# A hybrid decoder layer on one core: in which order of tokens the S5 gating path keeps its rows

## The reference

```python
proj = x @ w_in[l]
q, fz, iv, g, u = jnp.split(proj, ...)
o_a, sa = hgrn2_mixer(q, fz, iv, g, ...)          # gated linear recurrence, 4 heads
# inside s5_mixer, after the scan over the complex diagonal states:
y = y.reshape(B, T, D_S5) + d_skip * u
y = jax.nn.gelu(y, approximate=False)
o_b = y * jax.nn.sigmoid(y @ w_glu)
mix = jnp.concatenate([o_a, o_b], axis=-1) @ w_out[l]
x = layer_norm(ALPHA * x + mix, ln1_g[l], ln1_b[l])
x = layer_norm(ALPHA * x + conv_ffn(x, ...), ln2_g[l], ln2_b[l])
```

## Time and profile before

| what | value |
|---|---|
| median of 3 runs | 1214.69 us |
| the profiled execution, its own time | 1211.78 us |
| its span (first to last instruction) | 1210.1 us |
| granted TensorE clock, mean | 0.997 |
| TensorE busy | 97% of the span |
| VectorE busy | 67% |
| ScalarE busy | 42% |

### The profile page before, as it was taken

The page is one execution under the profiler, slowest core; times in us unless marked ns, Lnnn a source line. Parts: engine busy times, 40 slices in busy tenths (PEclk is TensorE's granted clock), DMA queues, the critical chain, the costliest instruction groups (busy, mean ns, idle before and its releaser), DMA issues.

```text
span 1210.1 us, 24082 instructions
## 1 busy us (share of the span) xinstructions
PE 1172.3 (97%) x9716; PEld 1129.5 (93%) x9716; DVE 815.3 (67%) x1517; ACT 509.1 (42%) x852; POOL 167.8 (14%) x138
## 2 busy tenths in 40 slices
PE   7999999998898999999999999999999999999996
PEld 7988889997787999998999999999999999999995
DVE  6995777657877557799627863686458743886555
ACT  5411212436755535765414541354225522554335
POOL 4210000100000233300210021001200020001452
PEclk9999999999999999999999999999999999999999
DMA  8431333528334410411272227222631265122512
GB/s 294 120 119 49 90 93 104 177 72 208 117 101 184 176 36 1 166 42 42 72 281 88 56 64 271 94 68 54 242 128 54 56 204 180 40 73 55 193 46 96
DMA packets 84815, 139.31 MB, mean 115 GB/s; under 512 B 26360, under 2 KB 52504, under 8 KB 84696
## 3 DMA queue, kind: packets, MB, share of 16 engines
q1 hardware_dynamic: 84704, 137.77, 35.7%
HBM read 97.89 MB, written 40.03 MB: 114 GB/s over the span
## 4 chain that ended last, share of the span: by engine, by line
PE 86%; DVE 8%; ACT 3%; issue 2%; DMA 1%; SPq 0%; ACTq 0%; DVEq 0%
PE psum L1905 31%; PE psum L1600 15%; PE psum L1877 15%; PE psum L1988 6%; PE psum L1619 6%; PE psum L1674 4%; PE psum L1589 1%; DVE XL L2137 1%; DVE R L2504 1%; PE psum L1727 1%; PE psum L1709 1%; DVE wl L2552 1%; PE psum L1722 1%; PE psum L1794 1%; PE psum L1795 1%
## 5 line engine op out<-in xcount | busy, mean ns | idle before, releaser
L1905 PE MATMUL psum<-XH,wh 128*128 128x258 f32 x640 | 181.3, 283 | 1.7 <-ACT ub L1305 1.4
L1905 PE MATMUL psum<-XH,wl 128*128 128x258 f32 x640 | 181.0, 283 | 0.0
L1905 PE MATMUL psum<-TR,wh 128*128 128x258 f32 x640 | 180.9, 283 | 0.0
L1905 PE MATMUL psum<-XL,wh 128*128 128x258 f32 x640 | 179.9, 282 | 0.0
L1551 POOL TENSOR_TENSOR wl<-raw,wh 128x512 fp32r<-128x512 f32 (+2 forms) x36 | 57.9, 1612 | 567.7 <-ACT wh L1254 557.1
L1877 PE MATMUL psum<-AH,wl 128*128 128x344 f32 x384 | 123.1, 320 | 0.0
L1877 PE MATMUL psum<-AL,wh 128*128 128x344 f32 x384 | 123.1, 320 | 0.0
L1905 PEld LDWEIGHTS psum<-XH,wh 128*128 128x128 f32 x640 | 121.0, 189 | 2.2 <-issue 2.2
L1877 PE MATMUL psum<-AH,wh 128*128 128x344 f32 x384 | 122.9, 320 | 0.0
L1905 PEld LDWEIGHTS psum<-XL,wh 128*128 128x128 f32 x640 | 121.5, 190 | 0.1
L1905 PEld LDWEIGHTS psum<-XH,wl 128*128 128x128 f32 x640 | 120.9, 189 | 0.0
(11 more groups left out here) (390 smaller groups left out, 2798.2 us busy)
## 6 DMA issues: line engine op xcount, KB each, us to landing
raw<-in_w_up SPq DMA_DIRECT2D x44, 512.0 KB, 3.9
ub<-rscr SPq DMA_DIRECT2D x16, 516.0 KB, 5.0
rscr<-ub SPq DMA_DIRECT2D x16, 516.0 KB, 3.9
raw<-in_w_dn SPq DMA_DIRECT2D x32, 256.0 KB, 3.2
raw<-in_w_units SPq DMA_DIRECT2D x15, 512.0 KB, 4.6
fscr<-st SPq DMA_DIRECT2D x10, 516.0 KB, 3.3
R<-in_xT SPq DMA_DIRECT2D x8, 516.0 KB, 6.6
RS<-rscr SPq DMA_DIRECT2D x8, 516.0 KB, 4.6
```

The source lines that it names most:

```text
L1905: ins = nc.tensor.matmul(psum[:, bank, 0:QW], a[:, k * P:(k + 1) * P], x, start=(start and p_ == 0), stop=(stop and p_ == 2), skip_group_c ...
```

## The change

y, the sigmoid's result and their product now stay in step order, and so do XH and XL rows 0 to 3 while they hold y. The copy `gelu c`, the split `gl c` and the product `z c` read and write runs of 128 contiguous values. The step from step order to token order is made in `zh c` and `zl c`, which each become two instructions: 1024 values read with 512 bytes from one to the next, and the 8 sample values.

```diff
-        ys = [x[:, :].rearrange("p (t n) -> p n t", t=L) for x in (*st, ybuf)]
+        ys = [x[:, :].rearrange("p (t n) -> p t n", t=L) for x in (*st, ybuf)]
...
+        def by_step(ap):
+            return ap.rearrange("p (t n) -> p t n", t=L)
+        def token_order(ap):
+            return ap.rearrange("p (t n) -> p n t", t=L)
+        def as_tokens(ap):
+            return ap.rearrange("p (n t) -> p n t", t=L)
...
                 elif kind == "zh":
                     act.wait_ge(z_ready, c + 1)
-                    me(act.activation(XH[:, HEADS + c, :], zb[c], ACT.Copy), z_hi)
+                    me(act.activation(as_tokens(XH[:, HEADS + c, 0:TP]), token_order(zb[c][:, 0:TP]), ACT.Copy))
+                    me(act.activation(XH[:, HEADS + c, TP:T], zb[c][:, TP:T], ACT.Copy), z_hi)
...
-                    me(act.activation(XH[:, c, 0:TP].rearrange("p (n t) -> p n t", t=L), ys[c][:, NS:NS + NL, :], ACT.Copy))
-                    me(act.activation(XH[:, c, TP:T], ys[c][:, 0:NS, 0], ACT.Copy), g_hi)
+                    me(act.activation(by_step(XH[:, c, 0:TP]), ys[c][:, :, NS:NS + NL], ACT.Copy))
+                    me(act.activation(XH[:, c, TP:T], ys[c][:, 0, 0:NS], ACT.Copy), g_hi)
...
             def z_split(m):
                 dve.wait_ge(z_hi, m + 1)
-                me(split(XL[:, HEADS + m, :], zb[m], XH[:, HEADS + m, :]), z_lo)
+                me(split(as_tokens(XL[:, HEADS + m, 0:TP]), token_order(zb[m][:, 0:TP]), as_tokens(XH[:, HEADS + m, 0:TP])))
+                me(split(XL[:, HEADS + m, TP:T], zb[m][:, TP:T], XH[:, HEADS + m, TP:T]), z_lo)
...
-                    me(split(n_t(XL[:, c, 0:TP]), ys[c][:, NS:NS + NL, :], n_t(XH[:, c, 0:TP])))
-                    me(split(XL[:, c, TP:T], ys[c][:, 0:NS, 0], XH[:, c, TP:T]), g_lo)
+                    me(split(by_step(XL[:, c, 0:TP]), ys[c][:, :, NS:NS + NL], by_step(XH[:, c, 0:TP])))
+                    me(split(XL[:, c, TP:T], ys[c][:, 0, 0:NS], XH[:, c, TP:T]), g_lo)
...
-                    me(TT(n_t(zb[m][:, 0:TP]), ys[m][:, NS:NS + NL, :], n_t(zb[m][:, 0:TP]), ALU.mult))
-                    me(TT(zb[m][:, TP:T], ys[m][:, 0:NS, 0], zb[m][:, TP:T], ALU.mult), z_ready)
+                    me(TT(by_step(zb[m][:, 0:TP]), ys[m][:, :, NS:NS + NL], by_step(zb[m][:, 0:TP]), ALU.mult))
+                    me(TT(zb[m][:, TP:T], ys[m][:, 0, 0:NS], zb[m][:, TP:T], ALU.mult), z_ready)
```

More of the change, by code:

```diff
@@ L2415, in _ @@
                     dve.wait_ge(g_hi, c + 1)
-                    n_t = lambda a: a.rearrange("p (n t) -> p n t", t=L)
-                    me(split(n_t(XL[:, c, 0:TP]), ys[c][:, NS:NS + NL, :], n_t(XH[:, c, 0:TP])))
-                    me(split(XL[:, c, TP:T], ys[c][:, 0:NS, 0], XH[:, c, TP:T]), g_lo)
+                    me(split(by_step(XL[:, c, 0:TP]), ys[c][:, :, NS:NS + NL], by_step(XH[:, c, 0:TP])))
+                    me(split(XL[:, c, TP:T], ys[c][:, 0, 0:NS], XH[:, c, TP:T]), g_lo)
                 elif kind == "ml":
```

## The result

| | before | after |
|---|---|---|
| median of 19 runs each | 1212.66 us | 1215.16 us |
| ratio, 95% interval | | 1.0023 [1.0014, 1.0031] |
| profiled execution, its own time | 1211.78 us | 1216.15 us |
| its span | 1210.1 us | 1214.4 us |
| its mean granted clock | 0.997 | 0.993 |

The change makes the kernel 0.23% slower, about 2.5 us in the medians. 1214.1 us was forecast and 1215.16 came, inside the range, but the step from before was off: +0.9 us was worked out and +2.5 came.

A forecast was written before the change was run, and what follows sets the result against it. TensorE, busy 97% of the span, was taken to bound the kernel; -2.0 (entry) + 1.05 (`zh 1`) + 0.9 (`zl 2`) + 0.95 (`zh 3`, `zl 3`) = +0.9 on 1213.2 gave 1214.1 us, range 1209.5 to 1219.0.

The forecast's parts named there:

- Prices: Per-instruction costs on ScalarE and VectorE: `gelu` 1.06 us, `gl` and `z` 1.23, strided `zh` and `zl` 2.1.
- The fifth rival: Runs of 128 don't read faster, so the entry gains nothing: about +4.4 us, 1217.6 us; 5% chance.
- the fourth: Rival: strided reads at 512 bytes' distance far dearer, 4.2 us a pair: +9.3 us, 1222.5 us; 5% chance.
- The VectorE terms: VectorE's strided-against-contiguous costs, nil by the skill's rule; forecast went by the trace, 2066 against 1233 ns.
- The entry: 311 to 337 us: shorter `gelu 2` and `gelu 3` bring TensorE's wait for K and later work 2.0 us earlier.
- 1.05 given back by `zh 1`: 354 to 373 us: strided `zh 1` in ScalarE's unbroken chain delays TensorE's RMS wait at 364.82 by 1.05 us.
- 0.9 given back by `zl 2`: 354 to 373 us: strided `zl 2` costs 0.9 us more, leaving the XH row 6 part level with before.
- 0.9 lost by `zh 3` and `zl 3`: 373 to 386 us: both strided, they delay level 6 and bring `kt 3` at 385.6 instead of 384.71.
- the rival in which the end hides it: Cheaper strided `zh 3` or slack in level 6 keeps the gain: down to -2.0, 1211.2 us; 10% chance.
- a second fall: Rival: wider TensorE gaps from 371 to 386 us drop the clock there too: +2.6 us, 1215.8 us; 15% chance.
- the clock is spared: Rival: shorter gaps before 335 us avoid the clock fall near 337 us: -0.8 us, 1212.4 us; 25% chance.
- The range: 1209.5 to 1219.0 us, from cases 1211.2 to 1215.8, run scatter 2.2 either side and strided-price bounds of 1.2.

The follow-up runs named there:

- e11: The changed kernel run again, unedited, beside runs of the kernel before; mean +2.6 us over before, ratio 1.0021.
- e5: The changed kernel with only `zl` contiguous as before, `zh` strided; mean +0.7 us over the kernel before, ratio 1.0007.
- e6: The changed kernel with only `zh` contiguous as before, `zl` strided; mean +0.5 us over the kernel before, ratio 1.0009.
- e2: The kernel before with only `zh` and `zl` made strided in two instructions; mean +7.5 us over before, ratio 1.0059.
- e7: The changed kernel with the last strided split, `zl 3`, on GpSimd instead of VectorE; mean +0.6 us over the kernel before, ratio 1.0006.
- e1: The changed kernel with both `zh` and `zl` contiguous as before (entry alone); mean -2.2 us against the kernel before, ratio 0.998.
- e9: The changed kernel with the return to token order made in `z`, `zh` and `zl` contiguous; mean -1.7 us against before, ratio 0.9988.
- e8: The changed kernel with throwaway matmuls ahead of level 7 of head 3 and `kt 3`; mean +1.6 us over before, ratio 1.0009.

## Why the prediction was right or wrong

- **Prices.** Right, for all six kinds of instruction, to 0.1 us. The fifth rival (runs of 128 don't read faster) and the fourth (dearer at 512 bytes) fall with them. The VectorE terms are not nil either: its strided split takes 2041 ns and its contiguous one 1219.
- **The entry, -2.0 us.** -2.27 in the table of stretches, -2.28 again in e11. It came out of three waits and not only out of the one for K that was named: K from 1.58 to 0.60 us, the wait of 0.68 us for level 7's QP at 327.35 to nothing, and one called "issue" near 320 us from 1.36 to 0.85. K did not come at 329.7 but at 331.63, since a fall near 303 us and the start had put 2.2 us in front of it; the RMS product and `kt 3` were late against the forecast for the same reason.
- **1.05 given back by `zh 1`.** 365.80 - 336.95 = 28.85 us against 27.80 from the earlier trace rows: 1.05.
- **0.9 given back by `zl 2`.** From `kt 2` to that part 35.60 us before, 37.45 after: 1.85 for both steps together, where 1.95 was worked out.
- **0.9 lost by `zh 3` and `zl 3`.** `kt 3` is 2.85 us further from `kt 2` than before; 2.9 was worked out. So the rival in which the end hides it falls. e5, e6 and e2 confirm the parts with 1.39, 2.10 and 3.74 us where 1.5, 2.0 and 3.8 were expected.
- **The clock: the step that failed.** The sum had no term for the clock: it kept the falls as they were in one execution of before, and gave "a second fall" 15%, at +2.6 us and 1215.8. In the runs after loses 2.5 us more of full speed than before, worth 1.5 to 2.2 of the 2.7 us between the means. That is the part of the result that the forecast lacks; the mechanism of the order of tokens, with its +0.9, held to within the noise. That the measured +2.5 us equals that rival's value is luck. The profiled execution had two more falls, one right behind the gaps from 371 to 388 us, where the rival saw it, and one near 303 us, among gaps that the change leaves alone (their waits are 0.40, 0.73, 1.23 and 0.88 us in both kernels). The median is over executions of which each has falls of its own. That a fall strikes in one execution and not in the next was not in the forecast at all. Nor does "the clock is spared" hold as a rule: after has the fall near 337 us and e11 does not, and without it the stretch to `kt 3` is 1.34 us shorter, not 1.7.
- **Why the changed kernel has more falls is open.** TensorE's waits from 371 to 388 us grew from 3.0 to 4.8 us, as forecast. e2, e5, e6 and e7, which all have a part of the return, lost 1.6 to 2.4 us more than before, and e1 and e9, which don't, only 0.9 and 0.7. But e11, with the whole return, lost only 1.2, and with intervals of about 1.2 us these are not told apart. e8 says that filling the end alone does not cure it.
- **The range.** Its own terms give 1209.0 (1211.2 less 2.2) for the lower end, where 1209.5 is stated.
- **The size of "no change".** The bound of 0.5% was too wide for this kernel: the interval of 19 runs is 0.1% to either side.

## What to carry to other kernels

Moving a strided access along a chain of engines doesn't remove it: look where it is paid already, and what stands behind it in the queue of the engine that gets it. Here it went from steps with slack in part into a chain ScalarE - VectorE - TensorE without any, and doubled, since one product became a high and a low part; left in the product, it costs what it cost before (2.03 against 2.01 us) and the gain is kept. When an edit moves waits of TensorE, count the clock falls over many runs on both sides before an order is blamed or praised.

## What the runs showed of the hardware

- The clock falls of one program are not fixed: over 92 runs of the kernel before the mean granted clock went from 0.993 to 0.998, with 2 us of time between 0.998 and 0.996.
- In the profiled executions the falls in the middle sit in different places (near 303, 309, 320, 337, 367 or 388 us). Most lost about 1.7 us of full speed; one of 8.00 us at 0.57 in e9, near 303 us, lost 3.4 and made its stretch 2.4 us longer. Where TensorE was busy through it, a fall of 1.7 us cost 1.6; where a wait followed, as in e11 near 367 us, 0.1.
- Strided fp32 pieces of 1024 values cost ScalarE 2.0 to 2.2 us (reads at 512 and 544 bytes' distance) and VectorE 2.0 to 2.2 (reads at 512 and 544, a write at 32); contiguous runs of 128 cost 1.05 and 1.22.
- A 2.93 us split on GpSimd stopped a VectorE product of 16 values for 2.7 us.
